# First expert begun in the mixer's program: five weight units, the token numbers and the tile tables, in a two-block transformer kernel

## The reference, cut to what matters

```python
h = h + jnp.concatenate([ret, pool], axis=-1) @ w_out[l]
h = h + moe(rms_norm(h, norm_moe_w[l]), router_w[l], router_b[l], ...)

def moe(hn, router_w, router_b, w_gu, b_gu, w_down, b_down):
    logits = xt @ router_w + router_b
    top_vals, top_idx = lax.top_k(logits, TOP_K)            # 4 of 32
    gates = jax.nn.softmax(top_vals, axis=-1)
    order = jnp.argsort(top_idx.reshape(-1)); tok = order // TOP_K
    gu = lax.ragged_dot(xt[tok], w_gu, group_sizes) + b_gu[sorted_e]
    gate, up = minimum(gu[:, ::2], 7.0), clip(gu[:, 1::2], -7.0, 7.0)
    act = (up + 1.0) * (gate * sigmoid(1.702 * gate))
    y = lax.ragged_dot(act, w_down, group_sizes) + b_down[sorted_e]
    out = zeros.at[tok].add(y * gates)
```

## Time and profile before

| | |
|---|---|
| median of 3 runs | 5382.48 us |
| the profiled execution's own time | 5380.71 us |
| its span, first to last instruction | 5378.6 us |
| TensorE busy | 5094.7 us (95%) |
| VectorE busy | 3268.8 us (61%) |
| ScalarE busy | 2190.6 us (41%) |
| GpSimd busy | 628.2 us (12%) |
| mean granted TensorE clock | 0.980 |
| moved to and from HBM | 938 MB, 174 GB/s |

### The profile page before, as it was taken

How to read it: one execution, slowest core, us unless ns; L and a number is a source line. 1 busy time by engine, 2 the same in 40 slices (tenths; PEclk the granted TensorE clock), 3 DMA queues, 4 the chain that set the end, 5 groups by cost and what they waited for, 6 DMA issues and landing times. The chain is left out here.

```text
span 5378.6 us, 78209 instructions
## 1 busy us (share of the span) xinstructions
PE 5094.7 (95%) x25188; PEld 3499.3 (65%) x25566; DVE 3268.8 (61%) x6237; ACT 2190.6 (41%) x3309; POOL 628.2 (12%) x862
## 2 busy tenths in 40 slices
PE   7999999799999999999999999979998899999698
PEld 4666665466666666666666666646665688887365
DVE  5444445577777777777777777754557544443266
ACT  4222222354544445555555555333332533333244
POOL 0000000100000000000000000011100399100000
PEclk9999999899999999999999999989999999999899
DMA  8777777665655657777777777453332400000533
GB/s 283 236 253 235 247 242 217 198 202 179 188 192 179 201 170 235 233 231 235 238 239 237 241 234 236 153 190 140 130 115 99 126 7 7 7 7 9 192 110 107
DMA packets 437589, 938.21 MB, mean 174 GB/s; under 512 B 61152, under 2 KB 86176, under 8 KB 436640
## 3 DMA queue, kind: packets, MB, share of 16 engines
q1 hardware_dynamic: 374816, 774.40, 44.1%
q10 hardware_dynamic: 35328, 87.57, 5.1%
q0 software_dynamic: 27280, 74.02, 4.3%
HBM read 781.97 MB, written 155.98 MB: 174 GB/s over the span
## 5 line engine op out<-in xcount | busy, mean ns | idle before, releaser
L1420 DVE TENSOR_TENSOR w_lo_gate<-stage,w_hi 128x1024 bf16<-128x1024 f32 (+1 forms) x800 | 929.8, 1179 | 188.9 <-ACT w_hi L1289 132.0
L1289 ACT ACTIVATE w_hi<-stage 128x1024 fp32r<-128x1024 f32 (+1 forms) x800 | 791.4, 1017 | 557.0 <-PE GU L1108 299.3
L1105 PE MATMUL GU<-w_hi,x_hl 128*128 128x512 f32 x2048 | 860.8, 420 | 16.5 <-DVE x_hl L1425 10.5
L1106 PE MATMUL GU<-w_hi,x_hl 128*128 128x512 f32 x2048 | 811.7, 396 | 0.0
L1108 PE MATMUL GU<-w_lo_gate,x_bf 128*128 128x512 bf16 x1920 | 479.8, 380 | 7.7
L1105 PEld LDWEIGHTS GU<-w_hi,x_hl 128*128 128x128 f32 x2048 | 387.0, 189 | 132.3 <-issue 32.9
L1105 PE MATMUL Y<-w_hi,a_hl 128*128 128x512 f32 x1024 | 456.7, 446 | 1.7 <-DVE a_hl L1431 1.7
L1106 PEld LDWEIGHTS GU<-w_hi,x_hl 128*128 128x128 f32 x2048 | 388.0, 189 | 83.0
L1106 PE MATMUL Y<-w_hi,a_hl 128*128 128x512 f32 x1024 | 404.4, 395 | 0.0
L1108 PEld LDWEIGHTS GU<-w_lo_gate,x_bf 128*128 128x128 bf16 x2048 | 174.4, 98 | 254.5 <-issue 88.4
L2915 DVE TENSOR_REDUCE ntop<-SC 128x1 f32<-128x2048 f32 x64 | 146.7, 2292 | 268.0 <-PE SC L3028 268.0
(11 more groups left out here) (635 smaller groups left out, 9178.4 us busy)
## 6 DMA issues: line engine op xcount, KB each, us to landing
stage<-in_expert_w_gate_up_dram SPq DMA_DIRECT2D x512, 512.0 KB, 5.2
stage<-in_expert_w_down_dram SPq DMA_DIRECT2D x224, 512.0 KB, 5.5
mixer_stage<-w_in_lo SPq DMA_DIRECT2D x150, 512.0 KB
mixer_stage<-in_w_out_dram SPq DMA_DIRECT2D x65, 512.0 KB, 9.3
expert_rows<-zero_y SPq DMA_DIRECT2D x64, 512.0 KB
mixer_stage<-w_out_rows SPq DMA_DIRECT2D x64, 512.0 KB
b_gu<-in_expert_b_gate_up_dram ACTq DMA_DIRECT2D x128, 256.0 KB, 4.8
expert_rows<-acted ACTq DMA_DIRECT2D x64, 512.0 KB, 3.3
```

What stands on the lines that cost most here:

```text
L1105: pe.matmul(out, high(k), w_high(k), start=(k == first), stop=False)
L1106: pe.matmul(out, low(k), w_high(k), start=False, stop=False)
L1289: act.activation(w_hi[:, c, ks, :], staged, ACT.Copy).then_inc(s["hi_done"], 1)
L1420: dve.tensor_tensor(w_lo[:, c, ks, :], staged, w_hi[:, c, ks, :], ALU.subtract).then_inc(s["lo_done"], 1)
```

## The change

The first expert's start is moved into the mixer's program, at the point where `order` is known.

- The sync engine waits for `order` between its stores of tiles 8 and 9 and issues the loads of the first expert's units 0 to 4 there; in the experts' program it begins with unit 5.
- GpSimd, at the end of its list in the mixer, waits for the scatter and for `order` and fetches the first expert's token numbers; in the experts' program the first gather finds them there.
- VectorE makes the tile tables right behind `order`, in the mixer; `tables()` goes.
- In the experts' program ScalarE's first list is written anew: `high` of units 0 to 3, one bias load, `x_high(0)`, then `high` of 4 to 7 with the other bias loads between them. VectorE's `x_low(0)` stands behind `low` of unit 3, not of unit 4.
- So that the units can land in the mixer, `stage` lives through the whole kernel. `mixer_stage` is now a name for it, and buffers of the second block (`probs`, `cos4`, `sin4`, `toep2`, `yT`, `x2_6`, `y_in`, `a_in`, `gain_post`) are laid into it; the instructions that use them are the same.

```diff
@@ -152,7 +152,7 @@
...
-        stage = sb("mixer_stage", [P, 5 * 1024])
+        stage = on_stage(S["stage"], 0, 5 * 1024)
@@ -418,7 +418,14 @@
...
             store_hn(TILES - 1)
-            for t in range(3, TILES):
+            for t in range(3, 9):
+                store_small(t)
+            sp.wait_ge(s["order_ready"], 1)
+            e = sp.value_load(S["order"][0:1, bass.ds(0, 1)], min_val=0, max_val=E - 1)
+            for m, (c, k0, k1) in enumerate(UNITS[0:STAGES]):
+                w = I["expert_w_gate_up"][0, bass.ds(e, 1), k0 * P:k1 * P, c * BANK:(c + 1) * BANK].squeeze(0)
+                sp.dma_start(S["stage"][:, m, 0:k1 - k0, :], w.rearrange("(k p) n -> p k n", p=P)).then_inc(S["st_in"][m], 16)
+            for t in range(9, TILES):
                 store_small(t)
@@ -462,6 +469,16 @@
...
             with pool.Fori(0, TILES) as t:
                 body(t)
+            pool.wait_ge(s["scattered"], 16 * TOPK * TILES)
+            pool.wait_ge(s["order_ready"], 1)
+            pool.sem_inc(s["lists_seen"], 1)
+            e = pool.value_load(S["order"][0:1, bass.ds(0, 1)], min_val=0, max_val=E - 1)
+            slot = nc.s_assert_within(pool.snap(e * CAP), 0, E * CAP - P,
+                                      skip_runtime_bounds_check_because="an expert has CAP places in the list")
+            for h in range(2):
+                pool.dma_start(S["ids"][h * HALF:(h + 1) * HALF, :],
+                               S["tok_list"][bass.ds(slot + h * HALF, HALF)]).then_inc(S["ids_in"], 16)
@@ -824,8 +841,8 @@
...
-            n_mid, is_long, upto, place, other = (stage[:, 4096 + n * E:4096 + (n + 1) * E] for n in range(5))
-            sel, picked = (stage[:, 2048 + n * E * E:2048 + (n + 1) * E * E].rearrange("p (i e) -> p i e", e=E) for n in range(2))
+            n_mid, is_long, upto, place, other = (c_all[:, n * E:(n + 1) * E] for n in range(5))
+            sel, picked = (vgu[:, n, 0:E * E].rearrange("p (i e) -> p i e", e=E) for n in range(2))
@@ -845,8 +862,19 @@
...
-            dve.tensor_copy(S["order"][:, :], other)
-            dve.tensor_copy(S["n_mid"][:, :], n_mid)
+            dve.tensor_copy(S["order"][:, :], other).then_inc(s["order_ready"], 1)
+            sorted_mid = is_long
+            ch.link(dve.tensor_tensor(picked, sel, row_of_e(n_mid), ALU.mult))
+            ch.link(dve.tensor_reduce(sorted_mid, picked, AX, ALU.add))
+            ch.link(dve.tensor_scalar(sorted_mid[:, 0:1], sorted_mid[:, 0:1], 1.0, None, ALU.max))
+            ch.link(dve.tensor_scalar(sorted_mid[:, E - 1:E], sorted_mid[:, E - 1:E], 1.0, None, ALU.max))
+            dve.tensor_copy(S["n_mid"][:, :], sorted_mid)
+            dve.memset(S["starts"][:, 0:1], 0)
+            dve.memset(S["rows64"][:, 0:1], 0)
+            for table, ends, more in (("starts", upto, 2.0), ("rows64", place, 4.0)):
+                ch.link(dve.tensor_scalar(other, sorted_mid, more, None, ALU.add))
+                ch.link(dve.tensor_tensor_scan(ends, other, zero_e[:, :], 0.0, ALU.add, ALU.add))
+                dve.tensor_copy(S[table][:, 1:E + 1], ends)
@@ -1185,8 +1213,6 @@
...
             first(0, 0)
-            eng.wait_ge(s["tables_ready"], 1)
-            eng.sem_inc(s["tables_seen"], 1)
             with eng.Fori(0, n_long) as i:
                 mids(i)
                 change(i)
@@ -1214,9 +1240,8 @@
...
             e = read(sp, "order", 0, E - 1)
-            for m in range(N_UNITS):
-                if m >= STAGES:
-                    sp.wait_ge(s["lo_done"], m - STAGES + 1)
+            for m in range(STAGES, N_UNITS):
+                sp.wait_ge(s["lo_done"], m - STAGES + 1)
                 load(m, e)
@@ -1234,13 +1259,10 @@
...
-            pool.wait_ge(S["scattered"], 16 * TOPK * TILES)
-            pool.sem_inc(s["ids_seen"], 1)
-
             def gather(slot, g, n):
 
 
-                for h in range(2):
+                for h in range(2 if slot is not None else 0):
...
             def first(i, g):
-                gather(slot_of(i, 0), g, P)
+                gather(None if is_step(i, 0) else slot_of(i, 0), g, P)
@@ -1394,13 +1416,16 @@
...
             act.sem_inc(s["y_stored"], 16)
-            for c in range(GU_CHUNKS):
+            for m in range(4):
+                high(0, m)
+            bias(0, 0)
+            x_high(0)
+            for c in range(1, GU_CHUNKS):
+                high(0, c + 3)
                 bias(0, c)
+            high(0, 7)
             bias_down(0)
-            for m in range(STAGES):
-                high(0, m)
-            x_high(0)
-            for m in range(STAGES, 16):
+            for m in range(8, 16):
                 high(0, m)
             experts(act, first, mid, last)
@@ -1517,31 +1542,6 @@
...
-            def tables():
...
-                tc.link(dve.tensor_tensor(sel, row_of_e(iota), row_of_i(order), ALU.is_equal))
-                tc.link(dve.tensor_tensor(picked, sel, row_of_e(n_mid), ALU.mult))
-                tc.link(dve.tensor_reduce(sorted_mid, picked, AX, ALU.add))
...
-                dve.sem_inc(s["tables_ready"], 1)
@@ -1618,11 +1618,10 @@
...
-            tables()
-            for m in range(STAGES):
+            for m in range(4):
                 low(0, m)
             x_low(0)
-            for m in range(STAGES, 14):
+            for m in range(4, 14):
                 low(0, m)
             experts(dve, first, mid, last)
@@ -3100,10 +3099,10 @@
...
-        toep = sb("toep2", [P, GS, P])
+        toep = on_stage(S["stage"], 0, GS * P).rearrange("p (g c) -> p g c", g=GS)
@@ -3229,13 +3228,13 @@
...
-        x2 = sb("x2_6", [P, 2, D])
+        a_in = on_stage(S["stage"], 3 * D, D).rearrange("p (u c) -> p u c", u=2)
+        x2 = on_stage(S["stage"], 0, 2 * D).rearrange("p (u c) -> p u c", u=2)
@@ -3602,6 +3601,10 @@
...
+            "stage": sb("stage", [P, STAGES, KP, BANK], F32),
+            "st_in": [ctx.enter_context(nc.semaphore(f"st_in{b}")) for b in range(STAGES)],
+            "ids": sb("ids", [P, 1], I32),
+            "ids_in": ctx.enter_context(nc.semaphore("ids_in")),
@@ -3630,18 +3633,16 @@
...
-            with ExitStack() as staged:
-                S["stage"] = staged.enter_context(nc.sbuf_tensor("stage", [P, STAGES, KP, BANK], F32))
-                expert_phase(nc, I, S)
-                combine_phase(nc, I, S)
+            expert_phase(nc, I, S)
+            combine_phase(nc, I, S)
...
-            with ExitStack() as latents:
-                held = lambda name, shape: latents.enter_context(nc.sbuf_tensor(name, shape, F32))
-                S.update({"probs": held("probs", [P, 2, SEQ]), "cos": held("cos4", [P, TILES, ROPE_HALF]),
...
+            turns = TILES * ROPE_HALF
+            S["probs"] = on_stage(S["stage"], 0, 2 * SEQ).rearrange("p (u c) -> p u c", u=2)
```

More of the change, by code:

```diff
@@ L1131, in expert_phase @@
         w_lo = S["w_lo_gate"]
-        stage = S["stage"]
+        stage, ids = S["stage"], S["ids"]
         b_gu = sb("b_gu", [P, 2 * FF])
@@ L1156, in expert_phase @@
             bg_in3 bd_in hi_done lo_done gu_ps gu_taken gate_ready tanh_ready acted_ready aT_ps a_hi_ready a_ready y_ps y_taken
-            y_stored y_seen dve_chain pool_chain tables_ready tables_seen table_chain low_free""".split()
+            y_stored y_seen dve_chain pool_chain table_chain low_free""".split()
         s = {n: sem(n) for n in names}
-        st_in = [sem(f"st_in{b}") for b in range(STAGES)]
+        st_in = S["st_in"]
         bg_in = [s[f"bg_in{c}"] for c in range(GU_CHUNKS)]
@@ L1163, in expert_phase @@
         ctx.callback(clear_semaphores, nc, dict(s))
-        s.update({n: S["keep"].enter_context(nc.semaphore(n)) for n in ("ids_in", "rows_in")})
+        s.update({n: S["keep"].enter_context(nc.semaphore(n)) for n in ("rows_in",)})
+        s["ids_in"] = S["ids_in"]
         block = ctx.enter_context(nc.Block())
@@ L1519, in numbers @@
                 tc.link(dve.tensor_scalar(iota, iota, -1.0, None, ALU.add))
-            def tables():
-                part = lambda n: w_lo[:, GU_CHUNKS + n // 2, n % 2 * 4:n % 2 * 4 + 4, :].bitcast(F32).rearrange("p k (i e) -> p (k i) e", e=E)
-                sel, picked = part(0), part(1)
-                iota, zero, order, n_mid, sorted_mid, cnt_t, ends_t, cnt, ends = (pre[:, n * E:(n + 1) * E] for n in range(9))
-                numbers(iota, zero)
-                tc.link(dve.tensor_copy(order, S["order"][:, :]))
-                tc.link(dve.tensor_copy(n_mid, S["n_mid"][:, :]))
-                tc.link(dve.tensor_tensor(sel, row_of_e(iota), row_of_i(order), ALU.is_equal))
-                tc.link(dve.tensor_tensor(picked, sel, row_of_e(n_mid), ALU.mult))
-                tc.link(dve.tensor_reduce(sorted_mid, picked, AX, ALU.add))
-                tc.link(dve.tensor_scalar(sorted_mid[:, 0:1], sorted_mid[:, 0:1], 1.0, None, ALU.max))
-                tc.link(dve.tensor_scalar(sorted_mid[:, E - 1:E], sorted_mid[:, E - 1:E], 1.0, None, ALU.max))
-                dve.tensor_copy(S["n_mid"][:, :], sorted_mid)
```

(17 more changed lines are left out.)

13 lines of the change are left out of this document (5 added, 8 removed).

## The result

The kernel after takes 5354.6 us (5349.16 to 5359.31, 5 runs), before beside it 5382.11 (5380.03 to 5384.93, 5 runs): ratio 0.9946, 95% interval [0.9933, 0.9959], 27.5 us less. The forecast was 5369, range 5364 to 5377. The profiled execution took 5354.6 us too, its span is 5352.6 against 5378.6. So 26.0 us of span went where 13.2 were forecast.

What follows compares the result with a forecast made beforehand. At the seam the kernel was taken to be bound by transfers that could not start before 986.7. The start 13.2 us earlier, other terms 0, gave 5367.5 for the profiled execution, 5369 for the median; range 5364 to 5377.

Steps and rivals of the forecast that it cites:

- the moved buffers of the second block change addresses only: 0: Term for the relocated second-block buffers: different addresses, no effect on time, 0 us.
- the 0.2% of the prediction's line: Whole kernel: smallest change a measurement tells, 10.8 us, so faster means below 5371.7; chance of faster 0.62.
- The mixer's end: I took 0: End of the mixer with five loads more: it ends when it did, 0 us, bounds 0 and 5.5 us.
- rival three: Mixer's end: loads slightly in the stores' way, 5.5 us back, gain 7.7, time 5375; chance 0.09.
- The gather: 4.9 us taken: First expert's row gather: issued near 987.0, rows at 991.9, from the median landing of 4.5 us plus 0.4.
- Rival two: First gather at the seam stays slow, 8.4 us: rows at 995.4, gain 9.5 us, time 5373; chance 0.10.
- almost to itself: First gather: unit 5's load follows only at 988.3, so the gather has the DMA engines nearly alone.
- The supply: 1015.0: Seam: unit 16 copied at 1015.0, engines at 387 GB/s, so chunk 3 begins at 1018.7, 13.3 us earlier.
- rival one: Seam: supply at the old mean of 291 GB/s sets it, unit 16 at 1018.9, time 5373; chance 0.11.
- Rival four: Mixer's end: loads much in the stores' way, end 14.6 us later, time 5384; chance 0.06.
- a gather whose issue VectorE locks out: First gather's issue on GpSimd beside VectorE's `low`: by the page, 2.5 us later, gain 10.5 us.
- 1.4 us more for a gather beside a stream of units: First gather sharing DMA engines by packet turns: loses at most half the rate, 1.4 us more, gain 11.8 us.

Runs made afterwards that it cites:

- e1: Kernel before with only the `ids` buffer allocated ahead of `w_hi`, which starts 32 bytes higher, no instruction moved: 5347.74 us, ratio 0.9965 to before.
- e2: Kernel after with `w_hi` put back to its old start 87328 and `x_hl` kept where it was: 5359.87 us, ratio 0.9989 to before.
- e3: Kernel after with `x_hl` moved 32 bytes higher and `w_hi` left in place: 5361.29 us, ratio 0.9989 to before.
- h3: Kernel after with both `w_hi` and `x_hl` 32 bytes lower, their distance kept: ratio 0.9952 to before.
- g2: Kernel after with the five weight loads issued behind the last of the mixer's stores: ratio 0.9952 to before.
- g1: Kernel after with the sync engine waiting for the first gather's rows before it loads unit 5: ratio 0.9945 to before.
- g3: Kernel after with ScalarE's and VectorE's first lists as in the kernel before (all biases first, `x_high` behind unit 4): ratio 0.9947 to before.
- h1: Kernel after with all five bias loads between ScalarE's copies of units 0 to 4 and `x_high` behind them: ratio 0.9943 to before.

## Why the prediction was wrong

**The step that failed** is "the moved buffers of the second block change addresses only: 0", with "all that follows on this chain is the same code". The allocation that moved `stage` also moved `w_hi` of the experts, by 32 bytes, which I had not looked at; the same code then ran 19.9 us shorter. e1 shows that this alone does it, e2 and e3 that without it the change is worth 0.9989, about 6 us, h3 that it is the distance of two buffers. That the kernel got faster is in part the forecast's mechanism, but that it got faster by more than the 0.2% of the prediction's line is luck: with the distance of before (e2) the ratio is 0.9989. Had the addresses stayed, the forecast's 13.2 would have been too high by 4 to 8 us.

**The seam** gave 5.2 and not 13.3. Unit 16, on which chunk 3 rests, was copied at 1023.2 and not at 1015.0. These 8.2 us, of which the last term is the remainder, are three terms:
- *The mixer's end: I took 0.* The gather was issued at 990.16 and not at 987.0. Of the 3.2 us, 0.9 is the mixer itself (last copy over at 980.1, before 979.2), but not the loads: `order` is written 0.9 later already (958.71, before 957.80), ahead of the first of them. 1.7 is the time from that copy to GpSimd's first instruction (8.2, before 6.5), just as much as the last store is waited for longer (4.5, before 2.8), and 0.6 is what stands between the identity and the issue, over what I counted. The 1.7 is rival three, and smaller than its 5.5 us: 339 GB/s were moved there, not the 229 by which I counted. In the ten kernels with the same schedule that time is 6.4 to 7.9 (the wait for the last store 2.7 to 4.2), so the price is 0 to 1.7 us. g2 doesn't avoid it (8.8): there the issue of the five loads, 3.1 us, stands behind the last store.
- *The gather: 4.9 us taken, 7.6 measured*, 7.1 to 7.5 in the ten. Rival two, with 2.7 of its 3.5 us, but not by its mechanism: units 5 to 8 were issued from 990.88 on, beside it, and without them it takes 5.3 (g1). I had said that the gather has the engines "almost to itself" until 988.3, but it was issued later than I thought, and the units with it.
- *The supply: 1015.0 was 2.3 us short*, on top. I counted from unit 9's load on 16.7 us to the copy of unit 16, with the engines at 387 GB/s; it took 19.0, with the engines full at 323. This is rival one's mechanism, a lower rate, though not by its number: the mean of 264 over the seam contains the empty part. I had added the bias loads to the bytes but not asked what the new list does with them: four of the five stand behind `x_high`, where they meet the second gather and the units (208 GB/s from 1004 to 1007, at a share of 0.93). The same list puts unit 4's copy behind the rows, and with it the load of unit 9. g3 and h1 show some 3 us for the two together.

**What was right.** ScalarE's first copy had its unit at once. Chunk 1 was not late: 6.97 us behind chunk 0, which has the 7.86 of before less some of its slow clock. From turning to first product it was 4.36 us again. Rival four, the stores delayed by 14.6 us, did not come. The Trainium skill's page "SBUF — State Buffer", section "SBUF: two separate sides", was cited for a gather whose issue VectorE locks out; the issue took 1.46 us beside `low` and 1.05 in g3, where VectorE does nothing yet, so what VectorE costs it is 0.4 us (0.7 in before and e1, with an issue of 1.77) and not 2.5; it is the landing that is late. By the Trainium skill's page "DMA: Bandwidth & Descriptors", section "Queues, rings and completion order", I had estimated 1.4 us more for a gather beside a stream of units; measured are 2.3 (7.6 in after, 5.3 in g1): the rule has the right side, and the measured cost is over half as much again. Each of the three terms was on record as a rival with a chance of about 0.1, as if one excluded the others; all three came together, each in part.

## What to carry to other kernels

A moved allocation is an edit of everything behind it: list the start of each buffer before and after, and price the inner products by what their buffers' distance does, with an experiment that moves only the distance. Compare two traces at several places over the whole span first; a gain that grows evenly over unchanged code is not the edit's mechanism. Where several transfers are brought forward to one point, add up the rivals that share the engines there and don't choose between them.
